# Gathered value rows summed on GpSimd instead of VectorE, with routing rounds written out and all first-layer rows gathered in the first layer

## The chip, the cores and the metric

The kernel runs on one core of one Trainium2 chip. The metric is the device time of one execution in microseconds; lower is better. PE is TensorE, DVE is VectorE, ACT is ScalarE, POOL is GpSimd and SP is SyncE, whose queue carries the weight loads.

## What is computed

A decoder block on 256 tokens of width 2048 in float32. The change touches only its last part, the expert channel mixer ("peer"). Each token and head picks 16 of 16384 experts by product keys. Each expert has one row in `u_tab` (first layer) and one in `v_tab` (second layer):

```python
s1 = einsum('thd,hnd->thn', qp[..., :half], sub_k1)      # 128 scores
s2 = einsum('thd,hnd->thn', qp[..., half:], sub_k2)      # 128 scores
v1, i1 = top_k(s1, 16);  v2, i2 = top_k(s2, 16)
cand = (v1[..., :, None] + v2[..., None, :]).reshape(T, 8, 256)
vals, flat = top_k(cand, 16)
experts = i1[flat // 16] * 128 + i2[flat % 16]
gates = softmax(vals)
hid = gelu(einsum('cd,chkd->chk', x, u_tab[experts]))
out = einsum('chk,chkd->cd', gates * hid, v_tab[experts])
```

## The kernel before

**Two ways for the tokens.** For 224 of the 256 tokens both expert layers are computed densely on PE: every expert's row is used for every token, and a table of gates that is zero for experts not picked selects. For the other 32 tokens (G = 32) the picked rows are gathered from HBM by indices: 32 tokens x 128 picks = 4096 rows of each table, 128 at a time, so 32 gathers of 128 x 2048 of the u rows (GJ = 32, numbers 0 to 31) and 32 of the v rows (numbers 32 to 63). A gather is an indirect DMA that POOL issues (`gather`, L488). Each u gather is multiplied by the tokens' normalised input and summed along the row on DVE (`gathered`, L1792), which gives one dot product per row; each v gather is scaled by its weight (one number per partition) and added to `y_acc`, also on DVE (L1795 for the first, L1798 for the rest: a multiply and an add in one instruction).

**The two dense layers.** Each streams 128 units of 128 x 2048 weights (1 MB each) through SP's queue. ACT rounds a unit to `w_hi` (`hi_wide`, L575), DVE subtracts to get the remainder `w_lo` (`lo_wide`, L1392), and PE multiplies with both. Four slots of `w_hi`/`w_lo` exist (SPLIT = 4), so the split of unit n+3 starts when unit n starts. The loops run over i = 0 to 15, with eight units k = 0 to 7 in each.

**First layer** (`hidden`, PE lines L1255 and L1256). While units stream, DVE also does the routing for i = 0 to 7 (`route`, two of the 16 routing rounds in each i; for each round part 0 copies 256 scores `sc` to `s_now`, L1719, and takes the top 16 of the first half, L1701 to L1705; part 1 takes those of the second half; part 2 those of the 256 sums; part 3 turns positions into one-hot rows `hot`). POOL finishes each round (`lookup`, L471 to L476) and adds two product halves for every second unit (`hidden_sum`, L467). In i = 1 to 5 DVE runs this as a hardware loop with the round number in a register. From i = 8 (I_TAB) on DVE builds gate tables (`picks_hot`, L1748 and L1752), which PE multiplies out (L1282), and reduces gathered u rows at the slots `PRE_SLOTS`, 27 of them (PRE = 27), over two buffers (`pre_ring`).

**Second layer** (PE lines L1304 and L1305, from 1643.7 us). For each pair of units, number m, the right-hand operand is made first: DVE multiplies the activations `h_in` by the gates `g_tab` (L1803), ACT rounds the product to `w_ul` (L867), and DVE subtracts (L1806). The two halves of `w_ul` alternate, so this chain for pair m+1 runs while PE works on pair m, and PE's wait for it is `wlow_done`. DVE's program is in order: at even k a `w_lo`, then the chain's product and difference; at odd k a `w_lo`. ACT's is in order too: at even k a `w_hi`, then the chain's rounding; at odd k a `w_hi`. POOL waits at each m until the chain m-1 is done, then loads the next `h_in` (L459), at even m also the next `g_tab` (L462), and at some m gathers the next row into `ring` (three buffers). DVE takes gathered rows behind a `w_lo` at the slots `V_SLOTS`: the 5 remaining u rows and the 32 v rows, three in each i. Where PE needs `y_acc` is only the very end (`bank_turned`, wait for `ring_used` 64).

Of the kernel before, what the change touches and what calls it, by code (L numbers as in the profile page):

```python
# [69 lines left out]
PRE = 27  # L70
# [25 lines left out]
def hybrid_block(nc, io):  # L96

    ctx = ExitStack()
    with ctx:
# [253 lines left out]
        def _(pool):  # L353
# [196 lines left out]
        def _(act):  # L550
# [355 lines left out]
            for i in range(1):  # L906
                experts_out(i)
            experts_out(1, gelu=7)
            with act.Fori(2, U_IT // 2 - 1) as i:
# [1085 lines left out]
```

## Time and profile before

| | us |
|---|---|
| median of three runs | 2315.85 (2314.83 to 2316.34) |
| profiled execution, its own time | 2314.72 |
| its span in the trace | 2312.7 |
| first expert layer, PE's stretch in the trace | about 946 to 1643.7 |
| second expert layer | 1643.7 to about 2286 |
| tail after it | about 27 |

The trace is that of the execution of 2314.72 us; 2.0 us of it lie outside the span. A row of the page's fifth part or of a query by groups gives a source line, the engine, the operation, output and inputs, how many, busy time and mean duration, and then the engine's idle time in front of them with what ended it. A row of a timeline gives start, duration, engine, line, operation and, in brackets, idle time in front with its releaser.

### The profile page before, as it was taken

To read this page: it belongs to the slowest core of one execution; us is meant where nothing else is said; L and a number is where in the kernel's file an instruction comes from. 1 tells how busy PE (TensorE), PEld (TensorE's weight loads), DVE (VectorE), ACT (ScalarE), POOL (GpSimd) and SP (SyncE) were. 2 spreads that over 40 slices of the span, in tenths; PEclk is the share of its full clock that TensorE was granted. 3 is DMA by queue.
4 is the path that set the end of the run, shared out by engine and by line. 5 is a ranking of instruction groups with operands and counts; after the bars stand their busy time and mean duration, and the time that the engine had idled before them with its cause. 6 is when DMAs were issued, how large, how long until landed. Compare 5 with 4: busy or idle time off the path is not lost.

```text
span 2312.7 us, 36297 instructions
## 1 busy us (share of the span) xinstructions
PE 2278.0 (98%) x13406; PEld 2072.4 (90%) x13406; DVE 1684.5 (73%) x2065; ACT 1214.2 (53%) x1138; POOL 476.6 (21%) x430
## 2 busy tenths in 40 slices
PE   7999999999999999999999999999999999999997
PEld 6888888888888889999999999999999999899997
DVE  5544776565655555989889989897688888888765
ACT  5534555555454344666666666565544444444443
POOL 0001342100000000243344422222222322222000
PEclk9999999999999999999999999999999999999999
DMA  7756555545456656666666899998999999999882
GB/s 279 276 192 216 207 204 209 196 164 174 166 201 222 225 199 234 211 226 228 222 235 229 318 343 336 326 331 317 356 383 366 377 382 376 370 397 379 327 305 83
DMA packets 122281, 623.70 MB, mean 270 GB/s; under 512 B 12000, under 2 KB 40928, under 8 KB 61776
## 3 DMA queue, kind: packets, MB, share of 16 engines
q1 hardware_dynamic: 58752, 423.65, 49.8%
q0 software_dynamic: 25616, 156.65, 17.9%
q10 hardware_dynamic: 37824, 42.18, 5.1%
q8 instruction: 60, 0.98, 0.2%
q14 instruction: 29, 0.24, 0.0%
HBM read 576.29 MB, written 46.14 MB: 269 GB/s over the span
## 4 chain that ended last, share of the span: by engine, by line
PE 79%; DVE 12%; issue 6%; ACT 1%; DMA 1%; DVEq 0%; POOL 0%; ACTq 0%; SPq 0%; POOLq 0%
PE psum L1304 17%; PE psum L947 10%; PE psum L949 10%; PE psum L948 10%; PE psum L1255 9%; PE psum L1305 8%; PE psum L1256 4%; DVE w_lo L1392 4%; PE psum L1282 2%; PE psum L1081 1%; DVE s_now L1719 1%; PE psum L1042 1%; DMA w_raw<-in_w_units 1%; PE psum L1003 1%; DVE i_top L1705 1%
## 5 line engine op out<-in xcount | busy, mean ns | idle before, releaser
L1255 PE MATMUL psum<-h2T,w_hi 128*128 128x448 f32 x2048 | 646.0, 374 | 1.4 <-DVE w_lo L1392 1.4
L1304 PE MATMUL psum<-w_ul,w_hi 128*128 128x448 f32 x2048 | 643.2, 374 | 3.5 <-DVE w_ul L1806 3.5
L1256 PE MATMUL psum<-h2T,w_lo 128*128 128x224 f32 x2048 | 543.3, 265 | 0.0
L1305 PE MATMUL psum<-w_ul,w_lo 128*128 128x224 f32 x2048 | 541.2, 264 | 0.0
L1384 DVE TENSOR_TENSOR w_lo<-w_raw,w_hi 128x2048 fp32r<-128x2048 f32 x144 | 332.2, 2312 | 214.9 <-ACT w_hi L563 214.5
L1304 PEld LDWEIGHTS psum<-w_ul,w_hi 128*128 128x128 f32 x2048 | 384.1, 188 | 34.1 <-issue 4.2
L563 ACT ACTIVATE w_hi<-w_raw 128x2048 fp32r<-128x2048 f32 x144 | 275.5, 1913 | 264.1 <-DMA w_raw<-in_w_units 231.6
L1255 PEld LDWEIGHTS psum<-h2T,w_hi 128*128 128x128 f32 x2048 | 383.8, 187 | 33.5 <-issue 3.7
L1305 PEld LDWEIGHTS psum<-w_ul,w_lo 128*128 128x128 f32 x2048 | 390.7, 191 | 0.0
L1256 PEld LDWEIGHTS psum<-h2T,w_lo 128*128 128x128 f32 x2048 | 390.2, 191 | 0.0
L1392 DVE TENSOR_TENSOR w_lo<-w_raw,w_hi 128x2048 fp32r<-128x2048 f32 x128 | 295.5, 2310 | 65.5 <-ACT w_hi L575 62.5
L1392 DVE TENSOR_TENSOR w_lo<-raw_x,w_hi 128x2048 fp32r<-128x2048 f32 x128 | 297.1, 2327 | 62.5 <-ACT w_hi L575 58.8
L947 PE MATMUL psum<-w_hi,hT_hi 128*128 128x512 f32 x768 | 306.1, 399 | 12.7 <-DVE w_lo L1384 12.7
L949 PE MATMUL psum<-w_hi,hT_lo 128*128 128x512 f32 x768 | 300.1, 391 | 0.0
L948 PE MATMUL psum<-w_lo,hT_hi 128*128 128x512 f32 x768 | 299.6, 390 | 0.0
L575 ACT ACTIVATE w_hi<-w_raw 128x2048 fp32r<-128x2048 f32 x128 | 244.5, 1913 | 82.4 <-PE psum L1305 36.9
L575 ACT ACTIVATE w_hi<-raw_x 128x2048 fp32r<-128x2048 f32 x128 | 243.4, 1907 | 49.4 <-PE psum L1305 28.7
L867 ACT ACTIVATE w_ul<-h_in 128x896 fp32r<-128x896 f32 x64 | 61.0, 954 | 271.3 <-DVE h_in L1803 271.3
L467 POOL TENSOR_TENSOR hs<-hs 128x448 f32<-128x448 f32 x64 | 110.7, 1730 | 385.4 <-ACT hs L856 378.7
L947 PEld LDWEIGHTS psum<-w_hi,hT_hi 128*128 128x128 f32 x768 | 144.7, 188 | 42.2 <-issue 14.0
L949 PEld LDWEIGHTS psum<-w_hi,hT_lo 128*128 128x128 f32 x768 | 144.5, 188 | 31.1
L948 PEld LDWEIGHTS psum<-w_lo,hT_hi 128*128 128x128 f32 x768 | 144.9, 189 | 28.4
(334 smaller groups left out, 2815.0 us busy)
## 6 DMA issues: line engine op xcount, KB each, us to landing
w_raw<-in_w_units SPq DMA_DIRECT2D x272, 1024.0 KB
raw_x<-in_w_units SPq DMA_DIRECT2D x128, 1024.0 KB, 6.7
g_tab<-tab_scratch POOLq DMA_DIRECT2D x32, 896.0 KB, 8.5
h_in<-hid_scratch POOLq DMA_DIRECT2D x64, 448.0 KB
hid_scratch<-hst ACTq DMA_DIRECT2D x32, 448.0 KB, 4.5
tab_scratch<-gate_a ACTq DMA_DIRECT2D x14, 1024.0 KB, 7.0
proj_scratch<-evac ACTq DMA_DIRECT2D x24, 512.0 KB, 4.9
x_nat<-in_x POOLq DMA_DIRECT2D x2, 2048.0 KB, 9.3
```

Of the source, the lines that this page charges most:

```text
L467: pool.tensor_tensor(both, both, hs[:, q, :, NU:2 * NU], ALU.add).then_inc(hid_summed, 1)
L563: act.activation(w_hi[:, s % SPLIT, :], w_raw[:, s % RAW, :], ACT.Copy).then_inc(hi_done, 1)
L575: act.activation(w_hi[:, s % SPLIT, :], src, ACT.Copy).then_inc(hi_done, 1)
L947: pe.matmul(out, xh[:, kc0 + c, ts], rh, start=st, stop=False, skip_group_check=True)
L948: pe.matmul(out, xh[:, kc0 + c, ts], rl, start=False, stop=False, skip_group_check=True)
L949: ins = pe.matmul(out, xl[:, kc0 + c, ts], rh, start=False, stop=en, skip_group_check=True)
L1255: pe.matmul(psum[:, k % 4, 0:2 * NU].rearrange("p (a t) -> p a t", a=2), uh, h2T[:, c, :, G:S], start=c == 0, stop=False, skip_group_check ...
L1256: ins = pe.matmul(psum[:, k % 4, NU:2 * NU], ul, h2T[:, c, 0, G:S], start=False, stop=c == KC - 1, skip_group_check=True)
L1304: pe.matmul(psum[:, c, 0:2 * NU].rearrange("p (a t) -> p a t", a=2), w_hi[:, s, o:o + P], ul, start=first, stop=False, skip_group_check=True)
L1305: return pe.matmul(psum[:, c, 0:NU], w_lo[:, s, o:o + P], ul[:, 0, :], start=False, stop=False, skip_group_check=True)
L1384: dve.tensor_tensor(w_lo[:, s % SPLIT, :], w_raw[:, s % RAW, :], w_hi[:, s % SPLIT, :].bitcast(F32), ALU.subtract).then_inc(lo_done, 1)
L1392: dve.tensor_tensor(w_lo[:, s % SPLIT, :], src, w_hi[:, s % SPLIT, :].bitcast(F32), ALU.subtract).then_inc(lo_done, 1)
```

## The change

Four things are edited.

1. The routing rounds of i = 1 to 5 are written out on DVE instead of looped, and the copy to `s_now` is gone: the top-16 search reads `sc` itself.
2. All 32 u gathers are reduced in the first layer (PRE = 32). Five of them are taken early, during routing, at slots (5,3), (5,7), (6,3), (6,7) and (7,3), all through one buffer; the gather indices (`gather_rows`) are made at (4,2) instead of (6,0). POOL's loop is written out from i = 4 for that. The other 27 keep their slots.
3. The 32 v rows are scaled and summed by POOL (`row_added`) in two instructions: a multiply by the row's weight in place, and an add to `y_acc` (the first row needs the multiply alone).
4. `V_SLOTS` has 32 entries, two in each i (k = 1 and 5) and a third (k = 7) in i = 2, 6 and 10; they only say at which m POOL takes a row and gathers the next. DVE takes no rows in the second layer. The gelu of the 32 dot products moves from unit (1,7) to (0,1) on ACT.

```diff
-PRE = 27
+PRE = 32
+PRE_EARLY = 5
...
+PRE_ISSUE = {(4, 3): 0, (5, 2): 1, (6, 0): 2, (6, 2): 3, (7, 0): 4}
+PRE_BUFFER = [0 if n < PRE_EARLY else (n - PRE_EARLY + 1) % 2 for n in range(PRE)]
-V_SLOTS = [(0, 5), (0, 7)] + [(i, k) for i in range(1, U_IT) for k in (1, 3, 5) if (i, k) != (2, 1)]
+V_SLOTS = sorted([(0, 5)] + [(i, k) for i in range(1, U_IT - 1) for k in (1, 5)] + [(2, 7), (6, 7), (10, 7)])
...
+            def row_added(n):
+                j = n % GJ
+                row = ring[:, (n - PRE) % RING, :]
+                if j == 0:
+                    pool.wait_ge(hidg_done, 1)
+                    pool.tensor_tensor(wts_g[:, :], hid_g[:, :], gsel[:, 2, :], ALU.mult).then_inc(hidg_done, 1)
+                    wait_alone(pool, hidg_done, 2)
+                pool.wait_ge(ring_in[(n - PRE) % RING], 16 * ((n - PRE) // RING + 1))
+                if j == 0:
+                    pool.tensor_scalar(y_acc[:, :], row, wts_g[:, 0:1], None, ALU.mult).then_inc(ring_used, 1)
+                else:
+                    pool.tensor_scalar(row, row, wts_g[:, j:j + 1], None, ALU.mult).then_inc(hidg_done, 1)
+                    wait_alone(pool, hidg_done, 2 + j)
+                    wait_alone(pool, ring_used, n)
+                    pool.tensor_tensor(y_acc[:, :], row, y_acc[:, :], ALU.add).then_inc(ring_used, 1)
...
+                    if (i, j) in PRE_ISSUE:
+                        pool.wait_ge(gidx_done, 1)
+                        gather(PRE_ISSUE[i, j])
...
-                if row < 2 * GJ and m in issue_at:
-                    gather(row)
-                    row += 1
+                if m in issue_at:
+                    row_added(added)
+                    added += 1
+                    if row < 2 * GJ:
+                        gather(row)
+                        row += 1
...
-                    if part == 0:
-                        step(dve.tensor_copy(s_now[:, :, :].rearrange("p a n -> p (a n)"), sc[:, ds(u, 1), :].rearrange("p a n -> p (a n)")), alone=True)
-                    top16(s_now[:, part, :], s_cut[:, part, :], v_top[:, part, :], i_top[:, part, :])
+                    top16(sc[:, u, part * PEER_NK:(part + 1) * PEER_NK], s_cut[:, part, :], v_top[:, part, :], i_top[:, part, :])
...
-                elif j == 0:
-                    dve.tensor_scalar(y_acc[:, :], row, wts_g[:, 0:1], None, ALU.mult).then_inc(ring_used, 1)
-                else:
-                    dve.wait_ge(ring_used, n)
-                    dve.scalar_tensor_tensor(y_acc[:, :], row, wts_g[:, j:j + 1], y_acc[:, :], ALU.mult, ALU.add).then_inc(ring_used, 1)
...
-            with dve.Fori(1, I_PICK0) as i:
-                step.enter(i, 1, 2 * ROUTE)
-                hidden(i, routes=True)
-                step.leave(I_PICK0 - 1)
-            for i in range(I_PICK0, I_TAB):
+            for i in range(1, I_TAB):
                 hidden(i, routes=True)
```

POOL in the second layer, before: `h_in` and `g_tab` are the pair's loads, `ring` is a gathered row.

```order
L459 DMA h_in<-hid_scratch 128x896
L462 DMA g_tab<-tab_scratch 128x1792
L459 DMA h_in<-hid_scratch 128x896
L488 DMA ring<-in_v_rows,gidx 128x2048
L459 DMA h_in<-hid_scratch 128x896
```

POOL at the same place in the changed program: `wts_g` holds the rows' weights, `y_acc` the running sum.

```order
L462 DMA h_in<-hid_scratch 128x896
L465 DMA g_tab<-tab_scratch 128x1792
L462 DMA h_in<-hid_scratch 128x896
L504 TENSOR_SCALAR ring<-ring,wts_g 128x2048
L507 TENSOR_TENSOR y_acc<-ring,y_acc 128x2048
L491 DMA ring<-in_v_rows,gidx 128x2048
```

A scaling and a sum have moved in front of the gather, and with it in front of the next pair's `h_in` load.

DVE in the second layer, before: `w_lo` is the remainder of a weight unit, `h_in` and `w_ul` are the operand chain of the pair.

```order
L1392 TENSOR_TENSOR w_lo<-w_raw,w_hi 128x2048
L1798 SCALAR_TENSOR_TENSOR y_acc<-ring,wts_g,y_acc 128x2048
L1392 TENSOR_TENSOR w_lo<-w_raw,w_hi 128x2048
L1803 TENSOR_TENSOR h_in<-h_in,g_tab 128x896
L1806 TENSOR_TENSOR w_ul<-h_in,w_ul 128x4x224
L1392 TENSOR_TENSOR w_lo<-raw_x,w_hi 128x2048 x2
```

DVE at the same place in the changed program.

```order
L1422 TENSOR_TENSOR w_lo<-raw_x,w_hi 128x2048 x2
L1813 TENSOR_TENSOR h_in<-h_in,g_tab 128x896
L1816 TENSOR_TENSOR w_ul<-h_in,w_ul 128x4x224
L1422 TENSOR_TENSOR w_lo<-w_raw,w_hi 128x2048 x2
L1813 TENSOR_TENSOR h_in<-h_in,g_tab 128x896
```

The row sums have left; the remainders and the operand chain stand as they did.

## Rows read from the trace of the kernel before

**Rows 1.** The page's busy times: engine, busy us, share of span, instructions.

```profile
PE 2278.0 (98%) x13406; PEld 2072.4 (90%) x13406; DVE 1684.5 (73%) x2065; ACT 1214.2 (53%) x1138; POOL 476.6 (21%) x430
```

**Rows 2.** Busy us by stretch: PE, PEld, DVE, ACT, POOL; clock, DMA share, GB/s.

```profile
960.00:1272.00 312.00, 310.64 (x1968) 293.69 (x1968) 281.85 (x587) 203.34 (x184) 132.28 (x107) 1.00 0.63 224
1272.00:1644.00 372.00, 371.21 (x2500) 356.14 (x2499) 319.52 (x387) 223.05 (x149) 95.95 (x67) 1.00 0.91 326
1644.00:1966.00 322.00, 321.20 (x2049) 306.12 (x2048) 258.66 (x158) 150.47 (x103) 85.25 (x75) 1.00 0.97 379
1966.00:2286.00 320.00, 317.30 (x2021) 301.94 (x2021) 241.46 (x146) 145.65 (x99) 54.43 (x58) 1.00 0.86 329
```

**Rows 3.** PE's waits: us in total, times, longest.

```profile
PE psum L1304 <- DVE w_ul L1806: 3.5, 5, 1.8
PE psum L1255 <- DVE w_lo L1392: 1.4, 5, 0.4
PE psum L1282 <- DVE hot2a L1752: 0.8, 1, 0.8
```

**Rows 4.** Timeline, one pair of the second layer without a gathered row: ACT, DVE, POOL.

```profile
2220.34 1.92 ACT L575 ACTIVATE w_hi<-w_raw 128x2048 fp32r<-128x2048 f32 x1 [1.99 <-PE psum L1305]
2225.62 0.95 ACT L867 ACTIVATE w_ul<-h_in 128x896 fp32r<-128x896 f32 x1 [3.36 <-DVE h_in L1803]
2226.48 1.90 ACT L575 ACTIVATE w_hi<-raw_x 128x2048 fp32r<-128x2048 f32 x1
2230.37 1.92 ACT L575 ACTIVATE w_hi<-raw_x 128x2048 fp32r<-128x2048 f32 x1 [1.99 <-PE psum L1305]
...
2222.29 2.29 DVE L1392 TENSOR_TENSOR w_lo<-w_raw,w_hi 128x2048 fp32r<-128x2048 f32 x1 [1.62 <-ACT w_hi L575]
2224.50 1.08 DVE L1803 TENSOR_TENSOR h_in<-h_in,g_tab 128x896 f32<-128x896 f32 x1
2226.61 1.09 DVE L1806 TENSOR_TENSOR w_ul<-h_in,w_ul 128x896 fp32r<-128x896 f32 x1 [1.02 <-ACT w_ul L867]
2228.41 2.29 DVE L1392 TENSOR_TENSOR w_lo<-raw_x,w_hi 128x2048 fp32r<-128x2048 f32 x1 [0.71 <-ACT w_hi L575]
...
2227.99 0.54 POOL L459 DMA_DIRECT2D h_in<-hid_scratch  x1 [8.96 <-DVE w_ul L1806]
```

**Rows 5.** Timeline, two places where POOL and DVE compute at once.

```profile
957.88 4.71 POOL L496 TENSOR_TENSOR g<-g,x_rep 128x2048 f32<-128x2048 f32 x1 [5.27 <-DMA x_rep<-x_scratch]
...
955.81 2.29 DVE L1392 TENSOR_TENSOR w_lo<-w_raw,w_hi 128x2048 fp32r<-128x2048 f32 x1 [0.17 <-DVE i_top L1705]
958.02 4.60 DVE L1724 CAST if_top<-i_top 128x32 f32<-128x32 uint32 x1
...
1140.41 1.16 POOL L467 TENSOR_TENSOR hs<-hs 128x448 f32<-128x448 f32 x1
...
1140.44 3.27 DVE L1392 TENSOR_TENSOR w_lo<-raw_x,w_hi 128x2048 fp32r<-128x2048 f32 x1 [0.24 <-DVE i_top L1705]
```

**Rows 6.** Timeline in a routing round: POOL's lookup and DVE's copy.

```profile
1257.30 3.21 POOL L471 TENSOR_TENSOR hot<-hot,if_top 128x512 f32<-128x512 f32 x1 [3.49 <-DVE hot L1734]
...
1257.07 2.28 DVE L1392 TENSOR_TENSOR w_lo<-raw_x,w_hi 128x2048 fp32r<-128x2048 f32 x1
1259.28 1.38 DVE L1719 COPY s_now<-sc 128x256 f32<-128x256 f32 x1
```

**Rows 7.** Timeline, an indirect gather beside a DVE subtraction, and one with DVE idle.

```profile
1684.03 2.73 POOL L488 DMA_INDIRECT ring<-in_u_rows,gidx  x1 [0.30 <-issue]
...
1683.61 2.29 DVE L1392 TENSOR_TENSOR w_lo<-raw_x,w_hi 128x2048 fp32r<-128x2048 f32 x1 [0.71 <-ACT w_hi L575]
...
1427.76 0.95 POOL L488 DMA_INDIRECT pre_ring<-in_u_rows,gidx  x1
```

**Rows 8.** Groups of DVE from 1080 us on: gathered rows.

```profile
L1798 DVE SCALAR_TENSOR_TENSOR y_acc<-ring,wts_g,y_acc 128x2048 f32<-128x2048 f32 x31 | 72.7, 2346 | 0.0
L1792 DVE CUSTOM_DVE_ANT_0 ring<-ring,g 128x2048 f32<-128x2048 f32 x5 | 11.4, 2285 | 0.0
```

More of the change, by code:

```diff
@@ L86, in bank_count @@
     return 2 * (KC // 2 - 1) + j + 1
-I_PICK0, I_TAB, I_PICK1, I_END = 6, 8, 9, 15
-PRE_SLOTS = [(I_TAB + (2 * n + 5) // 8, (2 * n + 5) % 8) for n in range(PRE)]
-V_SLOTS = [(0, 5), (0, 7)] + [(i, k) for i in range(1, U_IT) for k in (1, 3, 5) if (i, k) != (2, 1)]
+I_ROWS, I_PICK0, I_TAB, I_PICK1, I_END = 4, 6, 8, 9, 15
+PRE_SLOTS = [(5, 3), (5, 7), (6, 3), (6, 7), (7, 3)] + [(I_TAB + (2 * n + 5) // 8, (2 * n + 5) % 8) for n in range(PRE - PRE_EARLY)]
+PRE_ISSUE = {(4, 3): 0, (5, 2): 1, (6, 0): 2, (6, 2): 3, (7, 0): 4}
+PRE_BUFFER = [0 if n < PRE_EARLY else (n - PRE_EARLY + 1) % 2 for n in range(PRE)]
+V_SLOTS = sorted([(0, 5)] + [(i, k) for i in range(1, U_IT - 1) for k in (1, 5)] + [(2, 7), (6, 7), (10, 7)])
 VB = 4
@@ L481, in gather @@
                 if n < PRE:
-                    dst, landed, behind = pre_ring[:, n % 2, :], pre_in[n % 2], n - 1
+                    dst, landed, behind = pre_ring[:, PRE_BUFFER[n], :], pre_in[PRE_BUFFER[n]], n if n < PRE_EARLY else n - 1
                 else:
@@ L499, in _ @@
             pool.wait_ge(iota_in, 16)
-            with pool.Fori(0, I_TAB) as i:
+            with pool.Fori(0, I_ROWS) as i:
                 for j in range(4):
@@ L504, in _ @@
                         lookup(i * 2 + j // 2)
-            pool.wait_ge(gidx_done, 1)
-            pool.wait_ge(routed, ROUTES)
+            for i in range(I_ROWS, I_TAB):
+                for j in range(4):
+                    hidden_sum(i * 4 + j, j % 2)
+                    if j % 2 == 1:
+                        lookup(i * 2 + j // 2)
+                    if (i, j) in PRE_ISSUE:
+                        pool.wait_ge(gidx_done, 1)
+                        gather(PRE_ISSUE[i, j])
             for i in range(I_TAB, I_END):
@@ L509, in _ @@
                     hidden_sum(i * 4 + j, j % 2)
-                    if (i - I_TAB) * 4 + j < PRE:
-                        gather((i - I_TAB) * 4 + j)
+                    n = PRE_EARLY + (i - I_TAB) * 4 + j
+                    if n < PRE:
+                        if n == PRE_EARLY:
+                            pool.wait_ge(routed, ROUTES)
+                        gather(n)
             hidden_sum(4 * I_END, 0)
@@ L532, in _ @@
             issue_at = [4 * i + (k + 1) // 2 + 2 for i, k in V_SLOTS]
+            added = PRE
             for m in range(2, 2 * V_ROUNDS):
@@ L904, in gathered_gelu @@
                 act.activation(hid_g[:, :], dots[:, :], ACT.Gelu_apprx_tanh, scale=rs_g[:, 0:1]).then_inc(hidg_done, 1)
[L906 to L909, printed above, removed]
+            experts_out(0, gelu=1)
+            with act.Fori(1, U_IT // 2 - 1) as i:
                 experts_out(i)
@@ L1776, in gathered @@
             def gathered(n):
[L1778 to L1784 removed]
+                row = pre_ring[:, PRE_BUFFER[n], :]
+                dve.wait_ge(pre_in[PRE_BUFFER[n]], 16 * PRE_BUFFER[:n + 1].count(PRE_BUFFER[n]))
                 if n == 0:
                     dve.wait_ge(hg_done, 1)
[L1787 to L1798 removed]
+                dve.tensor_tensor_reduce(row, row, hg[:, :], 1.0, 0.0, ALU.mult, ALU.add, dots[:, n:n + 1]).then_inc(ring_used, 1)
             def weights(m, half):
@@ L1823, in hidden @@
                     lo_wide(i * 8 + (U0 + k + AHEAD), k + AHEAD)
-                    if k == 0 and isinstance(i, int) and i == I_PICK0:
+                    if (i, k) == (I_ROWS, 2):
                         gather_rows()
@@ L1865, in experts_out @@
                         weights(m, m % 2)
-                    if (i, k) in row_slots:
-                        gathered(row_slots[i, k])
-            row_slots = dict(zip(V_SLOTS, range(PRE, 2 * GJ)))
             def clear_tokens(h):
```

19 lines of the change are left out of this document (2 added, 17 removed).

## Prediction

> **What bounds the kernel now.** I read the page's busy times first, then the stretches, then PE's waits, then the timeline around one pair of units. PE is busy 2278.0 of 2312.7 us [rows 1], and in the two expert layers 1320.3 of 1326 us at the full granted clock, 1.00 [rows 2]. All that PE waits for DVE there is 3.5 + 1.4 + 0.8 = 5.7 us [rows 3]. So whatever this change takes off DVE can give back 5.7 us at most, 0.25% of the time. It can cost far more, since the engines that feed PE have little room in the second layer.
>
> How little is read from one pair [rows 4]. Let t = 0 be 2220.34, where ACT starts the rounding that it owes at the start of an even unit; the next pair starts at 10.03. DVE's remainder runs from 1.95 to 4.24, the product ends at 5.24, ACT's rounding at 6.23, the difference at 7.36, and PE needs it at 10.03. **The slack of the operand chain is 2.67 us.** At 7.65 POOL issues the next `h_in` load, until 8.19; DVE's odd remainder runs from 8.07 to 10.36. The next even remainder can start at 10.03 + 1.95 = 11.98.
>
> **What POOL and DVE do to each other.** An add of POOL over 128x2048 runs from 957.88 to 962.59 [rows 5]. It starts while a DVE subtraction still runs (to 958.10), and a DVE cast of 32 elements issued at 958.02 ends at 962.62, with the add. So the add had something to itself for 4.49 us from the end of the subtraction, and a tiny DVE operation waited all of it. The second place is the same with a DVE subtraction: 3.27 us instead of 2.29, ending about 2.1 us after POOL's 1.16 us add. I call this thing the port: one of the two holds it for a whole instruction. Who gets it next is in [rows 6]: POOL asked at 1257.30, DVE's subtraction ended at 1259.35, DVE's copy had been issued at 1259.28, and POOL went first: POOL ends at 1260.51, the copy at 1260.66. First asked, first served. The operations that this change meets in the second layer, remainder, product and difference, all read two SBUF tensors like the subtraction of [rows 5].
>
> **The change part by part.**
>
> *Value rows leave DVE.* 31 multiply-adds of 2.35 us and 5 dot products of 2.29 [rows 8], 84 us, leave the second layer's DVE. They stand behind PE, so this saves only the 3.5 us that PE waits for `w_ul` [rows 3].
>
> *Value rows come to POOL.* 31 adds at 4.49 us [rows 5] and 32 scalings. No row shows a scaling on POOL. From above it is bounded by the add, 4.49, which reads one tensor more. I take half of that, 2.25, since it reads one tensor and not two. Whether it needs the port is not shown either; the nearest row is the indirect gather, which reads one column of indices: alone 0.95 us, beside a subtraction 2.73 us [rows 7], ending 0.86 us after the subtraction's end at 1685.90. A single read of POOL waits for DVE too, so I take yes. From below its cost is then that of a scaling beside DVE's work, nothing, which is the first rival.
>
> Now one row, at a pair that starts at 0. POOL is ready to scale at about 8.3, behind its load. DVE's remainder has the port to 10.36; the scaling has it to 12.6; the next remainder (ready at 11.98) to 14.85; the add, ready at 12.8, was first in the queue and has it to 19.3. Only then the product, to 20.4, the rounding, to 21.4, and the difference, to 22.5. PE wants it at 20.06 and waits 2.45 us. After the first such row the odd remainder too comes late and the wait grows to what the port allows. Two pairs with one row need 4 x 2.29 + 4 x 1.09 = 13.5 us for DVE, 2.25 + 4.49 = 6.7 for POOL, and the gaps in which DVE waits for ACT, 2 x (1.02 + 0.71) = 3.5 [rows 4]: 23.7 us, where PE needs 20.06. **Each row costs 3.6 us.** At i = 2, 6 and 10 a third row follows in the next pair: there one pair carries a row, 6.75 + 6.74 + 1.73 = 15.2 against 10.03, 5.2 us each for six rows. The first row is a scaling alone and delays a remainder by 0.6 us, inside the slack: nothing. Sum: 24 x 3.6 + 6 x 5.2 + 2.45 = 120 us. It lies on PE's path, since nothing else covers a late `w_ul`.
>
> The Trainium skill ("GPSIMD Engine Reference", sections "4.1 Engine selection" and "3.1 Elementwise — side-by-side cycle accounting") calls GpSimd's one-input operations roughly line-rate, 1.03 cycles an element at 1.2 GHz: an estimate of 1.76 us for this scaling, and 0.49 us less for each of 31 rows, 105 us in place of 120. No row here shows a scaling on POOL. The same page's "8. Key points" names the contention: the interfaces are shared, and DVE instructions with two SBUF inputs or in a two-port mode meet it; [rows 5] agree, with 4.60 us for the cast.
>
> What is queued behind the row on POOL is the gather and the next `h_in` load, and behind that DVE's product. POOL is done with the row at 19.3, the gather at about 22, and the load is issued when the late difference is done, at 22.8; that `h_in` is wanted only a pair and a half later, so it isn't late.
>
> *Routing.* Each of the 16 rounds loses a copy of 1.38 us, of which some 1.1 us was waiting for POOL [rows 6]. Over i = 1 to 7 that is 14 x 1.38 = 19.3 us less for DVE, and the five early dot products add 5 x (2.29 + 0.08) = 11.8. DVE is busy 281.85 of 312 us there [rows 2] and PE waits for it 1.4 us, and 0.8 us at the first table [rows 3]. At best these 2.2 us go. At worst, if what the copies free in i = 1 to 4 isn't kept as lead, i = 5 to 7 stand at 11.8 - 6 x 1.38 = 3.5 us more, and PE waits for that before the first table. The remainders are made up to three units ahead, so lead is kept: I take -1.5, range -2.2 to +3.5. An early gather has about two units between issue and use; if it lands late, DVE waits in order and spends the same lead.
>
> *The rest.* Writing out the loop adds no work; the moved index making, the earlier gelu and the different buffer order shift small operations whose results have units of room. Nothing.
>
> **Sum.** +120 - 3.5 - 1.5 = +115 us. On the profiled execution, 2314.72, that is 2430; on the median, 1.1 us higher, 2431.
>
> **The rivals.**
>
> *The scaling needs no port.* It then runs beside the odd remainder and only the add blocks: 13.5 + 4.49 + 3.5 = 21.5 for two pairs, 1.4 us a row, and 12.97 for one, 2.9 us for six rows: 24 x 1.4 + 6 x 2.9 = 51, and with the other terms +46: 2362. For it speaks that no row shows a one-input computation waiting; against it the gather of [rows 7].
>
> *The scaling is as slow as the add.* 2.24 us more for each of 31 rows: 120 + 69 - 5 = +184, 2500. Against it speaks that it reads half as much.
>
> *POOL gives way (the other side).* If POOL's long add stood aside whenever DVE asks, the rows would fill DVE's idle time and cost PE nothing; PE's 5.7 us could go: 2311. It decides where POOL's uninterrupted hold falls below the slack of 2.67 us; between that and nothing gained lies "no difference". Against it stand both places of [rows 5], 4.49 us uninterrupted.
>
> *DVE's share of the add is smaller than the queue says,* because DVE's instruction, issued already, sometimes goes first, as the order of arrival is tight around 10.36 and 14.85. The sum over the port then still binds unless the gaps are filled: filled wholly, 13.5 + 6.7 = 20.2 against 20.06, close to nothing a row, 2320; half filled, 1.9 us a row and some 65 us in all, 2376.
>
> **How the numbers follow.** The queue with a scaling on the port, 2431 (between 2400 and 2475): 0.66. No port for the scaling, 2362: 0.13. Gaps partly filled, 2340 to 2400: 0.08. Slow scaling, around 2500: 0.05. POOL gives way, faster: 0.05. No difference: 0.03. A measurement of this kernel tells about 0.2% from no change, 4.6 us. The range 2355 to 2475 leaves out the slow scaling, the last two and part of the filled gaps. Faster 0.05, same 0.03, slower 0.92.
>
> **What would show it.** PE's wait for the difference in `w_ul` (was 3.5 us in 5 times) should be about 120 us in some 31 times of 2.5 to 5.2. The second layer should last some 755 us, not 640, the first layer within 3 us of before, at an unchanged clock. POOL's adds should stand at 4.5 us and more, the scalings at 2 to 4.5 with waiting, DVE's products and remainders in row pairs at 4 to 6 us where POOL holds. I am wrong if DVE's product keeps its 1.08 us beside POOL's add, if the scaling doesn't lengthen anything of DVE, or if PE waits for `w_lo` instead, which would mean that a chain I left out, the loads behind late remainders, comes last.

## The result, and the profile after

The changed kernel takes 2466.64 us (median of 4 runs, 2465.22 to 2467.52) where the kernel before took 2315.41 on the same chip: ratio 1.0649, interval 1.0637 to 1.0662, 151 us more. The predicted 2431 had the sign and the mechanism and was 36 us short.

In the changed kernel the lines have moved: the first layer's PE line L1255 is L1285, the second layer's L1304 and L1305 are L1334 and L1335, the remainder L1392 is L1422, the product L1803 is L1813, the difference L1806 is L1816, ACT's roundings L575 and L867 are L607 and L899, and POOL scales at L504 and adds at L507.

The page's busy times, to be held against [rows 1]:

```profile
PE 2337.5 (95%) x13406; PEld 2121.6 (86%) x13406; DVE 1831.6 (74%) x2016; ACT 1211.8 (49%) x1138; POOL 817.7 (33%) x494
```

Two numbers deserve a stop. DVE has 49 instructions fewer, with some 84 us of rows gone from the second layer, and is busy 147 us longer. PE has the same 13406 matmuls and is busy 59.5 us longer. DVE's "busy" holds waiting that the profile doesn't separate; PE's holds matmuls at the lower clock. By stretches, with the columns of [rows 2]:

```profile
960.00:1272.00 312.00, 310.61 (x1984) 296.04 (x1983) 277.21 (x581) 204.90 (x187) 145.59 (x113) 1.00 0.68 242
1272.00:1644.00 372.00, 369.89 (x2488) 354.40 (x2487) 318.50 (x386) 221.68 (x146) 96.02 (x67) 1.00 0.91 325
1644.00:2020.00 376.00, 332.89 (x1941) 312.67 (x1940) 310.69 (x122) 143.28 (x95) 230.43 (x97) 0.92 0.75 296
2020.00:2440.00 420.00, 369.32 (x2152) 346.78 (x2152) 343.16 (x143) 153.18 (x108) 238.00 (x96) 0.92 0.68 265
```

The first layer is as it was: PE's stretch in it lasts 701.1 us before and 700.5 now, to 1644.4. All the time is in the second, where PE got through 2049 matmuls in 322 us before [rows 2] and now through 1941 in 376. To the last matmul with `w_hi` the second layer took 650.7 us and takes 801.7, the whole 151. PE's waits, as in [rows 3]:

```profile
PE psum L1334 <- DVE w_ul L1816: 93.8, 32, 4.5
PE psum L1312 <- DVE hot2a L1778: 1.9, 1, 1.9
PE psum L1285 <- DVE w_lo L1422: 1.6, 2, 1.4
```

93.8 us are waits for the operand chain. The rest is in the matmuls: L1334 takes 399 ns in the mean, where its twin took 374 before. Groups of 1660 to 2440 us:

```profile
L1334 PE MATMUL psum<-w_ul,w_hi 128*128 128x448 f32 x1992 | 682.9, 399 | 93.0 <-DVE w_ul L1816 93.0
L1422 DVE TENSOR_TENSOR w_lo<-raw_x,w_hi 128x2048 fp32r<-128x2048 f32 x62 | 319.9, 5185 | 39.8 <-ACT w_hi L607 39.5
L504 POOL TENSOR_SCALAR ring<-ring,wts_g 128x2048 f32<-128x2048 f32 x31 | 189.8, 6122 | 1.1
L507 POOL TENSOR_TENSOR y_acc<-ring,y_acc 128x2048 f32<-128x2048 f32 x31 | 144.4, 4657 | 6.6 <-POOL ring L504 6.6
L1813 DVE TENSOR_TENSOR h_in<-h_in,g_tab 128x896 f32<-128x896 f32 x62 | 96.6, 1558 | 1.1 <-DMA h_in<-hid_scratch 1.1
L1816 DVE TENSOR_TENSOR w_ul<-h_in,w_ul 128x896 fp32r<-128x896 f32 x62 | 94.1, 1518 | 63.2 <-ACT w_ul L899 63.2
```

The 62 remainders from `raw_x`, two of the four in a cycle and the two that mostly meet POOL's row, take 5.19 us each where [rows 4] have 2.29: 180 us of DVE "work" that is standing still. POOL's queue isn't what is late: DVE waits only 1.1 us in all for `h_in` to land. And here is one settled cycle of two pairs with one row, POOL, DVE and ACT, from one late end of the chain (2106.40) to the next (2131.21):

```profile
2115.59 5.46 POOL L504 TENSOR_SCALAR ring<-ring,wts_g 128x2048 f32<-128x2048 f32 x1
2121.27 4.68 POOL L507 TENSOR_TENSOR y_acc<-ring,y_acc 128x2048 f32<-128x2048 f32 x1 [0.21 <-POOL ring L504]
...
2105.31 1.09 DVE L1816 TENSOR_TENSOR w_ul<-h_in,w_ul 128x896 fp32r<-128x896 f32 x1 [1.01 <-ACT w_ul L899]
2107.11 4.49 DVE L1422 TENSOR_TENSOR w_lo<-w_raw,w_hi 128x2048 fp32r<-128x2048 f32 x2 [0.71 <-ACT w_hi L607]
2111.53 1.08 DVE L1813 TENSOR_TENSOR h_in<-h_in,g_tab 128x896 f32<-128x896 f32 x1
2113.63 1.09 DVE L1816 TENSOR_TENSOR w_ul<-h_in,w_ul 128x896 fp32r<-128x896 f32 x1 [1.02 <-ACT w_ul L899]
2115.44 12.66 DVE L1422 TENSOR_TENSOR w_lo<-raw_x,w_hi 128x2048 fp32r<-128x2048 f32 x2 [0.71 <-ACT w_hi L607]
2128.02 1.08 DVE L1813 TENSOR_TENSOR h_in<-h_in,g_tab 128x896 f32<-128x896 f32 x1
2130.12 1.09 DVE L1816 TENSOR_TENSOR w_ul<-h_in,w_ul 128x896 fp32r<-128x896 f32 x1 [1.02 <-ACT w_ul L899]
...
2118.28 1.92 ACT L607 ACTIVATE w_hi<-raw_x 128x2048 fp32r<-128x2048 f32 x1 [2.88 <-PE psum L1335]
```

Two remainders beside POOL's two instructions take 12.66 us, not 4.49; the other two take 4.49. Nothing else in the cycle is longer. It lasts 24.8 us, where PE would need 20.06. In DVE's brackets ("idle before") there is only ACT: 1.02 + 0.71 + 1.02 + 0.71 us. ACT waits once for PE, but its rounding ends at 2120.20, while DVE is still at the remainder before, which alone lasts 6.04 us, until 2121.48. So no wait for PE reaches the end of the chain: **DVE, ACT and POOL form a loop of their own, and PE trails it.**

### The profile page after: what moved, and what is told of

Read it like the earlier page. It is cut to its first block, busy times and chain, and to the rows that moved or that the text cites. A ratio compares the mean times of both kernels' runs of the same rounds, so it can differ in the third digit from the quotient of the medians.

```text
span 2464.3 us, 36030 instructions
## 1 busy us (share of the span) xinstructions
PE 2337.5 (95%) x13406; PEld 2121.6 (86%) x13406; DVE 1831.6 (74%) x2016; ACT 1211.8 (49%) x1138; POOL 817.7 (33%) x494
## 4 chain that ended last, share of the span: by engine, by line
PE 69%; DVE 17%; issue 8%; ACT 4%; DMA 1%; DVEq 0%; ACTq 0%; POOL 0%; SPq 0%; POOLq 0%
PE psum L1285 15%; DVE w_lo L1422 10%; PE psum L977 10%; PE psum L979 10%; PE psum L978 10%; PE psum L1286 7%; PE psum L1334 6%; ACT w_hi L607 3%; DVE h_in L1813 3%; PE psum L1335 3%; PE psum L1312 2%; DVE w_ul L1816 1%; PE psum L1111 1%; ACT w_ul L899 1%; PE psum L1236 1%
## 5 line engine op out<-in xcount | busy, mean ns | idle before, releaser
L1334 PE MATMUL psum<-w_ul,w_hi 128*128 128x448 f32 x2048 | 701.1, 398 | 93.8 <-DVE w_ul L1816 93.8
L1285 PE MATMUL psum<-h2T,w_hi 128*128 128x448 f32 x2048 | 644.4, 373 | 1.6 <-DVE w_lo L1422 1.6
L1335 PE MATMUL psum<-w_ul,w_lo 128*128 128x224 f32 x2048 | 563.8, 275 | 0.0
L1334 PEld LDWEIGHTS psum<-w_ul,w_hi 128*128 128x128 f32 x2048 | 412.5, 201 | 136.6 <-DVE w_ul L1816 81.8
L1422 DVE TENSOR_TENSOR w_lo<-raw_x,w_hi 128x2048 fp32r<-128x2048 f32 x128 | 473.2, 3709 | 72.6 <-ACT w_hi L607 70.2
L1335 PEld LDWEIGHTS psum<-w_ul,w_lo 128*128 128x128 f32 x2048 | 419.0, 205 | 0.0
L1285 PEld LDWEIGHTS psum<-h2T,w_hi 128*128 128x128 f32 x2048 | 383.8, 187 | 31.6 <-issue 2.1
L1422 DVE TENSOR_TENSOR w_lo<-w_raw,w_hi 128x2048 fp32r<-128x2048 f32 x128 | 292.4, 2304 | 60.9 <-ACT w_hi L607 58.2
L607 ACT ACTIVATE w_hi<-raw_x 128x2048 fp32r<-128x2048 f32 x128 | 244.1, 1909 | 97.8 <-PE psum L1335 79.2
L607 ACT ACTIVATE w_hi<-w_raw 128x2048 fp32r<-128x2048 f32 x128 | 241.7, 1907 | 50.0 <-PE psum L1286 24.6
L899 ACT ACTIVATE w_ul<-h_in 128x896 fp32r<-128x896 f32 x64 | 60.9, 952 | 404.2 <-DVE h_in L1813 404.2
L504 POOL TENSOR_SCALAR ring<-ring,wts_g 128x2048 f32<-128x2048 f32 x31 | 189.8, 6122 | 1.1
```

Source lines behind the costliest of these rows:

```text
L504: pool.tensor_scalar(row, row, wts_g[:, j:j + 1], None, ALU.mult).then_inc(hidg_done, 1)
L607: act.activation(w_hi[:, s % SPLIT, :], src, ACT.Copy).then_inc(hi_done, 1)
L1285: pe.matmul(psum[:, k % 4, 0:2 * NU].rearrange("p (a t) -> p a t", a=2), uh, h2T[:, c, :, G:S], start=c == 0, stop=False, skip_group_check ...
L1334: pe.matmul(psum[:, c, 0:2 * NU].rearrange("p (a t) -> p a t", a=2), w_hi[:, s, o:o + P], ul, start=first, stop=False, skip_group_check=True)
L1335: return pe.matmul(psum[:, c, 0:NU], w_lo[:, s, o:o + P], ul[:, 0, :], start=False, stop=False, skip_group_check=True)
L1422: dve.tensor_tensor(w_lo[:, s % SPLIT, :], src, w_hi[:, s % SPLIT, :].bitcast(F32), ALU.subtract).then_inc(lo_done, 1)
```

## The experiments

The theory to test: one of DVE and POOL holds a port for a whole instruction, so a row costs the two holds less what slack is left. "Hold" is the time for which POOL keeps DVE from its operands; "duration" is the length of POOL's own record. Open were how long each instruction holds it, whether duration or hold counts, and what the lowered clock costs.

**The rows alone.** The changed kernel, with only the value rows given back to DVE, at the new `V_SLOTS`:

```diff
-                    row_added(added)
-                    added += 1
...
+                    if (i, k) in row_slots:
+                        summed(row_slots[i, k])
```

> The changed kernel with one part undone: the 32 value rows are summed on DVE again, at the new slots (two in an i, three in i = 2, 6 and 10); the written-out routing and the five early dot products stay. Port theory (POOL's scaling and add keep DVE from its operands, and nothing else costs): the whole of the 151 us goes, 2312 to 2318. Rival, that the first-layer edits or the gather order carry part of it: over 2330.

Measured: 2311.70 us, ratio to the kernel before 0.9981 (0.9972 to 0.9991). So the port theory stands: the value rows on POOL cost 155 us, and all the rest of the change together gains 4.7 us (2.1 to 6.5 by the interval). PE's wait for the operand chain here:

```profile
PE psum L1315 <- DVE w_ul L1811: 1.8, 3, 0.8
```

**Each instruction alone.** The sum without the scaling, and the scaling without the sum:

```diff
 add alone
-                    pool.tensor_scalar(row, row, wts_g[:, j:j + 1], None, ALU.mult).then_inc(hidg_done, 1)
...
 scaling alone
-                    pool.tensor_tensor(y_acc[:, :], row, y_acc[:, :], ALU.add).then_inc(ring_used, 1)
```

> The changed kernel without POOL's scaling: gathered value rows are added unscaled, so the weighting of these rows is left out. Port theory: two pairs need 13.5 us of DVE, 4.5 of POOL and 3.5 of gaps for ACT, 21.5 against 20.06, 1.4 us a row and 2.9 where two pairs in a row carry one: about +46, 2355 to 2372, PE's single waits 1 to 3 us. Clock theory (each wait of PE lets the granted clock fall and the slow matmuls add to the time): 20 us or more on top, over 2380.

> The changed kernel without POOL's add: rows are only scaled in place, so the sum of the value rows is left out. The scaling took 5.46 us even with DVE off SBUF, yet DVE's product came through about 3.4 us after its start. If it holds the port for those 3.4 to 3.7 us: 13.5 + 3.6 + 3.5 = 20.6 for two pairs, 0.5 us a row, 2 us in six: 2325 to 2345. If it holds it for all of its 5.46 us: 22.5, 2.4 us a row and 3.9 in six, 2380 to 2400.

Measured: 2358.40 us with the add alone (ratio 1.0180, 1.0159 to 1.0200), 2332.79 with the scaling alone (1.0069, 1.0049 to 1.0089). Both lie where the port theory had them. A hold of the full 5.46 us (2380 to 2400) fell, and so did the clock theory (over 2380): with the add alone PE waits for `w_ul` 31 times too, 36.5 us in all and 2.7 at most, and the granted clock over the span is 0.995. Over the 2311.70 of the experiment before that is 46.7 and 21.1 us; together they cost 155, more than twice the 68 of the two alone. The slack of a cycle of two pairs explains that, 20.06 - 13.5 - 3.5 = 3.1 us: each alone has it to itself, both together have it once. Two remainders beside a 5.48 us scaling, with no add, POOL and DVE of the scaling alone:

```profile
2101.27 5.48 POOL L504 TENSOR_SCALAR ring<-ring,wts_g 128x2048 f32<-128x2048 f32 x1
...
2101.11 8.26 DVE L1419 TENSOR_TENSOR w_lo<-raw_x,w_hi 128x2048 fp32r<-128x2048 f32 x2 [0.72 <-ACT w_hi L604]
```

DVE loses 8.26 - 4.49 = 3.8 us to an instruction of 5.48. So the scaling is longer than the add, but holds the port for less than its length.

**Holds by themselves.** A small kernel of its own, executed once: two equal instructions of POOL over 128x2048, alone and beside six dependent ones of DVE. The sections of POOL beside DVE's subtractions, and of POOL's scaling beside DVE's, come twice in it, with the same times.

> A measuring kernel of its own: nothing of the block is computed, the output is zeros. POOL runs each operation twice, alone and beside six dependent DVE operations: scaling by a pointer or by a constant, multiply by a broadcast weight, add, copy, of 2048 and 512 columns; DVE's are a subtraction of two SBUF tiles, a scaling, a subtraction with a PSUM operand and a max. Port theory: alone the scaling by pointer takes 5.46 us, add 4.5, copy about 2 to 3; beside the subtraction each POOL operation delays one DVE subtraction by its hold, add by 4.5, scaling by 3.4 to 3.7; the max and the PSUM subtraction are delayed by none. Rival, POOL slows every DVE operation by a rate: all of DVE's stretch a little.

POOL alone (scaling by a column, multiplication by the same column spread out, add x2, copy x2):

```profile
15.34 5.44 POOL L26 TENSOR_SCALAR pa<-pa,pw 128x2048 f32<-128x2048 f32 x1 [0.17 <-POOL pa L26]
39.10 7.34 POOL L32 TENSOR_TENSOR pa<-pa,pw 128x2048 f32<-128x2048 f32 x2 [0.24 <-DVEq L61]
49.14 9.13 POOL L35 TENSOR_TENSOR pb<-pa,pb 128x2048 f32<-128x2048 f32 x2 [0.24 <-DVEq L61]
61.41 3.91 POOL L38 COPY pb<-pa 128x2048 f32<-128x2048 f32 x2 [0.24 <-DVEq L61]
```

DVE: six subtractions alone; beside POOL's scaling, spread multiplication, add and copy; then, beside scalings, six of DVE's own scalings, six subtractions with a PSUM operand and six top-8 searches:

```profile
67.06 13.92 DVE L41 TENSOR_TENSOR dc<-da,db 128x2048 f32<-128x2048 f32 x6 [57.57 <-POOLq L61]
81.20 7.53 DVE L44 TENSOR_SCALAR dc<-da 128x2048 f32<-128x2048 f32 x6 [0.22 <-POOLq L61]
...
117.24 20.70 DVE L41 TENSOR_TENSOR dc<-da,db 128x2048 f32<-128x2048 f32 x6 [0.22 <-DVEq L88]
...
158.93 20.64 DVE L41 TENSOR_TENSOR dc<-da,db 128x2048 f32<-128x2048 f32 x6 [0.22 <-DVEq L88]
179.79 22.43 DVE L41 TENSOR_TENSOR dc<-da,db 128x2048 f32<-128x2048 f32 x6 [0.22 <-DVEq L88]
202.44 17.20 DVE L41 TENSOR_TENSOR dc<-da,db 128x2048 f32<-128x2048 f32 x6 [0.22 <-DVEq L88]
219.87 17.77 DVE L44 TENSOR_SCALAR dc<-da 128x2048 f32<-128x2048 f32 x6 [0.22 <-DVEq L88]
237.86 13.89 DVE L47 TENSOR_TENSOR dc<-da,ps 128x2048 f32<-128x2048 f32 x6 [0.22 <-DVEq L88]
251.97 13.94 DVE L50 MAX8 top<-da 128x8 f32<-128x2048 f32 x6 [0.22 <-DVEq L88]
```

DVE isn't slowed evenly, as the rival had it. The third of the six subtractions beside the scaling, and the last three:

```profile
125.28 5.68 DVE L41 TENSOR_TENSOR dc<-da,db 128x2048 f32<-128x2048 f32 x1
...
131.00 6.94 DVE L41 TENSOR_TENSOR dc<-da,db 128x2048 f32<-128x2048 f32 x3
```

The second and the third take 5.69 and 5.68 us, the other four 2.29. So each POOL instruction stops one subtraction, and half of what DVE loses is the hold of one POOL instruction against this subtraction:

| POOL instruction | alone, us | DVE's subtractions lose, us |
|---|---|---|
| scaling by a column | 5.44 | (20.70 - 13.92) / 2 = 3.4 |
| multiply by the spread column | 3.67 | (20.64 - 13.92) / 2 = 3.4 |
| add | 4.56 | (22.43 - 13.92) / 2 = 4.25 |
| copy | 1.95 | (17.20 - 13.92) / 2 = 1.6 |

DVE's own scalings, which read one SBUF tensor, lose (17.77 - 7.53) / 2 = 5.1 us to each of POOL's scalings, not 3.4. So the hold belongs to a pair of instructions, one on each engine; "port" is a name for what they share, and no row shows the part itself. The subtraction that reads PSUM and the search lose nothing: their 13.89 and 13.94 are their times alone.

**Duration or hold.** The two ways to scale hold alike and differ in length by 1.8 us. In the kernel:

```diff
-                    pool.tensor_scalar(row, row, wts_g[:, j:j + 1], None, ALU.mult).then_inc(hidg_done, 1)
+                    pool.tensor_tensor(row, row, wts_g[:, j:j + 1].to_broadcast([P, D]), ALU.mult).then_inc(hidg_done, 1)
```

> The changed kernel with POOL's scaling written as a tensor_tensor multiply by the weight broadcast along the row, which reads two inputs. Expected to take 4.5 us like the add and to hold the port for all of it. Port theory: the hold counts, 4.5 in place of some 3.6, so it is slower than the changed kernel although the instruction is shorter: 2480 to 2500. Rival, the duration on POOL counts: 1 us a row less, 2430 to 2445.

Measured: 2466.77 us, ratio 1.0647 (1.0626 to 1.0669): the same time as the changed kernel, so both expectations missed. POOL's groups from 1660 us on:

```profile
L507 POOL TENSOR_TENSOR y_acc<-ring,y_acc 128x2048 f32<-128x2048 f32 x31 | 197.3, 6366 | 6.3 <-POOL ring L504 6.3
L504 POOL TENSOR_TENSOR ring<-ring,wts_g 128x2048 f32<-128x2048 f32 x31 | 116.4, 3755 | 0.5
```

The scaling is 2.4 us shorter than in the changed kernel, the add behind it 1.7 us longer, and the cycle doesn't move. With the small kernel's 3.4 us for either form this leaves the hold, and not the duration, as what counts. I had written down a longer hold for this form because it has two inputs; that was wrong.

**Smaller pieces.** If holds compete with DVE's chain, shorter ones can slip into the 3.5 us of gaps. Each row in two halves of 1024 columns, scaling and add in turn:

```diff
+                    for q in range(PIECES):
+                        b = slice(q * (D // PIECES), (q + 1) * (D // PIECES))
+                        pool.tensor_scalar(row[:, b], row[:, b], wts_g[:, j:j + 1], None, ALU.mult).then_inc(hidg_done, 1)
...
+                        pool.tensor_tensor(y_acc[:, b], row[:, b], y_acc[:, b], ALU.add).then_inc(hidg_done, 1)
...
```

> The changed kernel with each row's scaling and add cut into halves of 1024 columns, in the order scale, add, scale, add: same columns, four shorter holds of about 1.8 and 2.3 us, each below the slack of 2.67 us. If what counts is the single hold against the slack: close to before, 2315 to 2340. If what counts is the sum of the holds over the port (DVE 13.5, POOL 8, gaps 3.5 in 20.06 us): no gain, 2450 to 2480.

Measured: 2400.67 us, ratio 1.0369 (1.0350 to 1.0388), between the two expectations, so both missed. A cycle of two pairs lasts 22.2 us, not 24.8: of the 4.7 us above PE's 20.06 some 2.6 are gone, the rest stays. DVE's four remainders in the cycle that ends at 2124.04:

```profile
2102.54 7.83 DVE L1427 TENSOR_TENSOR w_lo<-raw_x,w_hi 128x2048 fp32r<-128x2048 f32 x2 [0.71 <-ACT w_hi L612]
2114.19 6.73 DVE L1427 TENSOR_TENSOR w_lo<-w_raw,w_hi 128x2048 fp32r<-128x2048 f32 x2 [0.71 <-ACT w_hi L612]
```

They lose 3.34 + 2.24 = 5.6 us to four POOL instructions, where the whole ones cost 12.66 - 4.49 = 8.2. One by one: the two half adds cost 2.19 and 2.24 us, together what the whole add does (6.70 - 2.29 = 4.4). The saving is all in the scaling. Its second half costs DVE nothing: it is on POOL from 2108.21 to 2114.00, and the product and the difference in that stretch keep their 1.08 and 1.09. Its first half costs 3.43 - 2.29 = 1.1 us, where the whole scaling costs 6.04 - 2.29 = 3.75. So shorter instructions do slip into gaps, and a half scaling holds for less than half of a whole one; I had put 1.8 for it. And a wait appeared that the changed kernel doesn't have, at i = 2, 6 and 10, where three rows follow in neighbouring pairs. POOL and DVE at the first of them:

```profile
1807.54 0.59 POOL L463 DMA_DIRECT2D h_in<-hid_scratch  x1
...
1817.93 2.34 DVE L1818 TENSOR_TENSOR h_in<-h_in,g_tab 128x896 f32<-128x896 f32 x1 [9.12 <-issue]
```

The `h_in` load could have been issued at 1801.38, when the difference ended, but stands behind a row and its gather on POOL until 1807.54; the product starts 10.4 us later, which is also the median landing of these loads there. Three such waits of 9.1 to 9.2 us on DVE, 27.5 us, stand among the 89 us that this version still loses against the rows on DVE.

**What the low clock costs.** After each wait PE runs at about half clock for 3 us. Windows of 3 us in the changed kernel, granted clock behind the busy times:

```profile
2103.00:2106.00 3.00, 0.44 (x4) 0.16 (x2) 1.99 (x3) 1.67 (x2) 1.22 (x1) 1.00 0.42 142
2106.00:2109.00 3.00, 2.54 (x9) 2.37 (x10) 2.29 (x2) 2.88 (x2) 1.11 (x2) 0.55 1.03 434
2109.00:2112.00 3.00, 3.00 (x18) 2.86 (x18) 3.00 (x3) 0.00 (x0) 0.00 (x0) 0.88 0.98 399
2112.00:2115.00 3.00, 3.00 (x21) 2.86 (x21) 1.70 (x2) 2.35 (x2) 0.00 (x0) 1.00 1.03 434
```

That is the step from 2.4 to 1.2 GHz and back, once in 24.8 us. It looks like a cost of 50 us and more. To see whether it is one, PE was given twelve matmuls with a zero tile before every second wait for the chain:

```diff
+                    if k in (2, 6):
+                        zero = rs_diag[:, 1, :]
+                        for _ in range(FILL):
+                            pe.matmul(psum[:, 0, 0:P], zero, zero, start=False, stop=False, skip_group_check=True)
                     if k % 2 == 0:
                         pe.wait_ge(wlow_done, i * 4 + (k // 2 + 1))
...
```

Left out of the diff is where DVE sets the tile to zero and PE waits for that, once.

> The changed kernel with 12 matmuls of a zero tile (128x128, about 0.22 us each, 2.7 us, result unchanged) in front of PE's waits for the operand chain at k = 2 and 6, so that PE isn't idle while it waits. Theory that the lower clock is hidden (the loop of DVE, ACT and POOL sets 24.8 us for two pairs, and slow matmuls only shorten PE's next wait): clock near 1.00, time within 10 us of 2467. Clock theory: up to 58 us of slow matmuls go, 2410 to 2430.

Measured: 2469.11 us, ratio 1.0663 (1.0647 to 1.0679). The clock of both second-layer stretches rises from 0.92 to 0.97, short of the 1.00 expected, L1334's mean falls from 399 to 384 ns, the waits for `w_ul` fall from 93.8 to 48.6 us (part of them is now filled), and the time is what it was. The first of the two stretches:

```profile
1644.00:2020.00 376.00, 352.79 (x2287) 335.70 (x2286) 308.02 (x120) 143.03 (x95) 224.85 (x96) 0.97 0.74 293
```

The clock theory's 2410 to 2430 fell. What PE loses at the low clock it would otherwise lose waiting: a matmul that ends earlier only meets the late operand earlier.

**The routing edits alone, on the kernel before.** Rounds written out and copy gone; and rounds written out with the copy kept:

```diff
-                    if part == 0:
-                        step(dve.tensor_copy(s_now[:, :, :].rearrange("p a n -> p (a n)"), sc[:, ds(u, 1), :].rearrange("p a n -> p (a n)")), alone=True)
-                    top16(s_now[:, part, :], s_cut[:, part, :], v_top[:, part, :], i_top[:, part, :])
+                    top16(sc[:, u, part * PEER_NK:(part + 1) * PEER_NK], s_cut[:, part, :], v_top[:, part, :], i_top[:, part, :])
...
-            with dve.Fori(1, I_PICK0) as i:
...
+            for i in range(1, I_TAB):
```

> The kernel before with one part of the change alone: routing rounds written out and the copy of the scores gone; 27 early rows, 5 u rows and all value rows on DVE in the second layer as before. DVE loses 16 copies of 1.38 us where PE waits for it 1.4 us in all: 1 to 2 us faster than before, 2313 to 2315. Rival, the freed time is lost again to POOL's adds, which now meet DVE's subtraction: within 0.5 us of before.

> The kernel before with the routing rounds written out but the copy of 256 scores kept, all else as before. The routing edits together gave 4.8 us, more than the 2.2 us that the view of waits shows. Theory A: the gain is the copies', whose 14 x 1.38 us took DVE's lead at many small places, so this kernel stands within 1 us of the kernel before (2314.5 to 2316.5), and PE's matmul count in 940 to 1300 us stays near 2281. Rival B: the loop itself costs (instruction fetch, register work, waits at each turn), so this kernel keeps 2 us or more of the 4.8 (2310.4 to 2313.5), with some 2300 matmuls or more in that stretch.

Measured: 2310.43 us (ratio 0.9979, 0.9970 to 0.9988) and 2312.57 us (ratio 0.9984, 0.9975 to 0.9993): 4.8 us (2.8 to 6.9) and 3.4 us (1.6 to 5.8) faster than the kernel before. The first is more than the 1 to 2 us expected, so that expectation missed; the second is rival B's, the loop itself. The 1.4 us between them, the copies' share, is within the two intervals. In the traces the first layer lasts 701.1 us before, 696.0 with both edits and 697.7 with the loop written out alone. The stretch of 1000 to 1190 us, inside the looped part, of these three in this order:

```profile
1000.00:1190.00 190.00, 189.01 (x1196) 178.39 (x1195) 170.67 (x355) 123.40 (x111) 73.18 (x64) 1.00 0.63 229
...
1000.00:1190.00 190.00, 190.00 (x1215) 181.22 (x1214) 156.93 (x350) 125.71 (x113) 65.67 (x64) 1.00 0.65 231
...
1000.00:1190.00 190.00, 190.00 (x1215) 181.21 (x1214) 173.84 (x364) 125.98 (x115) 85.08 (x65) 1.00 0.66 231
```

PE's busy time says that 1.0 us can be won, its matmuls say more: 1215 in place of 1196, and 19 at 190 / 1215 = 0.156 us are 3.0 us. One of PE's waits of the kernel before shows what comes round there:

```profile
1072.71 0.44 PE L1255 MATMUL psum<-h2T,w_hi 128*128 128x448 f32 x1 [0.24 <-DVE w_lo L1392]
```

Four such waits stand 40.8 us apart (1031.89, 1072.71, 1113.54 and 1154.35), once in a turn of DVE's loop; each is 0.2 to 0.3 us as a wait and 0.75 us by the count. So most of what the late operand costs sat in matmuls that count as busy. Written out, both are gone, with the copies still there. What the copies add shows after the loop: with them PE still waits 1.0 us for `hot2a` at the first table, without them not at all. The copy gone with the loop kept wasn't tried. The version with both routing edits and all rows on DVE, 2310.43 us, beats both kernels; the rows on DVE at the new slots, with the early dot products (2311.70), can't be told from it.

## Why the prediction was right, and where it was short

**The mechanism** stands. DVE's losses with the rows on POOL, the cycle with no step of PE in it, and the 155 us that vanish when the rows go back to DVE are what it said. Its rule for who goes first, "first asked, first served", does not stand, as told below; no time of the loop hangs on it. Of its rivals, "POOL gives way" and "no port for the scaling" (2362) fell: the scaling alone costs 21 us, which it couldn't without the port. "As slow as the add" (2500) is the odd one: it was right on the duration, too low even, and wrong on the cost, because the hold is shorter than the duration. "Gaps partly filled" fell for whole rows; with half rows it is in part what happens. Its own figure was loose too: with half of the gaps filled a pair with its own row costs 6.75 + 6.74 + 0.87 - 10.03 = 4.3 us, so the sum is 24 x 1.9 + 6 x 4.3 + 2.45 = 74 us, not 65.

**The step that was mis-sized** is the scaling, 2.25 us, taken as half an add "since it reads one tensor and not two". It lasts 5.46 and holds the port for 3.4 by the small kernel, 3.75 by the 6.04 us of the remainder in the kernel. The bound from above, "the add, which reads one tensor more", wasn't a bound: the number of inputs doesn't order POOL's instructions, since the copy (one input) takes 1.95 and the scaling (one input and a column) 5.44. A value from the middle between two bounds that no row carries was a guess. The add's 4.49 was right within 0.25 (hold 4.25).

The page that I cited, "GPSIMD Engine Reference" of the Trainium skill, section "4.1 Engine selection", would have led further off: its roughly line-rate for one input gave an estimate of 1.76 us, against 5.46 measured; only the copy, 1.95, comes near that. Section "8. Key points" of the same page of the Trainium skill has contention with DVE instructions of two SBUF inputs or in a two-port mode. The small kernel agrees on the first: the subtraction of two SBUF tensors loses 3.4 us, the one with a PSUM operand nothing. DVE's scaling, with one SBUF input, loses 5.1; in which mode it ran no row shows.

With the measured holds the prediction's own sum reads: two pairs 13.5 + 3.4 + 4.25 + 3.5 = 24.6 us (24.8 measured), 4.6 a row, 24 x 4.6 = 110; a pair with its own row 6.75 + 7.65 + 1.73 = 16.1 against 10.03, 6 x 6.1 = 37; with 2.45 for the second row 149, less 5 makes +144, 2460. Measured are +151. So the formula, with holds measured in a kernel of their own, gives 95% of the cost, and one input of it was 1.15 us low, 31 times.

**Order.** "First asked, first served" fits the add of the cycle shown: at 2121.27 it found DVE at work until 2121.48, took 4.68 us, and the remainder begun at 2121.40 waited, 6.70 us. It doesn't fit the scaling. That begins at 2115.59, 0.15 us after the remainder, yet takes 5.46 us, about its time alone, and the remainder takes 6.04: the later one went first. The opposite stands at the neighbouring rows, POOL and DVE at i = 2:

```profile
1795.90 9.01 POOL L504 TENSOR_SCALAR ring<-ring,wts_g 128x2048 f32<-128x2048 f32 x1
...
1797.38 2.29 DVE L1422 TENSOR_TENSOR w_lo<-w_raw,w_hi 128x2048 fp32r<-128x2048 f32 x1
1799.59 4.53 DVE L1813 TENSOR_TENSOR h_in<-h_in,g_tab 128x896 f32<-128x896 f32 x1
```

The scaling had begun 1.5 us before this remainder and was passed by it; then the product waited. With the spread multiplication at the same place (begun 1795.68, remainder begun 1797.20) it is the remainder that waits, 5.69 us, so the kind of instruction has a part in it. POOL issues a load just in front of each scaling, from 2115.02 on in the cycle shown; whether that decides the first case is not shown, and what lets DVE pass in the second stays open. The sum of a cycle doesn't depend on the order, since both holds fall between two ends of the chain either way. The slack of 2.67 us can't be read from a cycle that has used it up. Where both holds met the two remainders, product and difference kept their 1.08 and 1.09; with the neighbouring rows their means rose to 1.56 and 1.52.

**Waits of PE.** I wrote about 120 us in 31 times of 2.5 to 5.2; it is 93.8 in 32, at most 4.5. The second layer was to grow by some 115 us and grew by 151. "At an unchanged clock" was wrong: it is 0.92 in the second layer. The two misses belong together. Of the 151 us, 90 show as more waiting and most of the rest as slower matmuls, (399 - 374) ns x 2048 = 51 us on L1334. Whoever had read only the waits would have found some 60 us missing, and would have sought them in a second cause; the filled waits show that the clock isn't one.

**The small terms.** -3.5 for the value rows off DVE and -1.5 for the routing were the forecast; the changed kernel with the rows on DVE gains 4.7 us, against 5. That this came out so near is in part luck: the interval is 2.1 to 6.5, and the parts were mis-sized. The traces place only some of it, since the two profiled executions differ by 1.6 us (2314.72 and 2313.14); there the second layer is 2.3 us shorter, 648.4 against 650.7. PE's stretch in the first layer is 0.6 us shorter in the changed kernel and 0.4 longer with the rows on DVE. It is 5.1 us shorter with the routing edits alone, where I had 2.2 as the most, since "writing out the loop adds no work" took no account of what the loop itself costs, and since "at best these 2.2 us go" took PE's waits for all of the loss. The rest of the first-layer edits, the five early dot products above all, takes 4.5 us back: the wait for `hot2a` grew from 0.8 to 1.9 us and one of 1.4 for `w_lo` came, at 1265 us. That DVE's lead is used up there is how I read it; no run has the early dot products alone. My bound of +3.5 assumed that no lead is kept, and was further off than -1.5.

**POOL's queue**: that the late load does no harm was right for the changed kernel and wrong in the version with halves, where it costs three waits of 9 us.

## What to carry to other kernels

Before moving work from DVE to POOL, add up on one line, for one period, DVE's instructions that meet POOL at the port (here those that read two SBUF tensors), POOL's holds, and DVE's gaps for other engines. Here that sum passed PE's period, 24.6 us against 20.06, and the excess was paid each time, while the page had DVE at 74% and POOL at 33%. Price a POOL instruction that no row shows by a small kernel, beside DVE and alone, since neither its number of inputs nor its length gives the hold. And where PE waits often, count its matmuls per stretch beside its busy time and its waits: here both of the latter hid late operands.

## What the hardware showed that was not expected

- POOL over 128x2048 in float32: scaling by a column 5.44 us, by a constant 5.36, multiplying by the same column spread out 3.67, add 4.56, copy 1.95. The slowest form is the one made for scaling.
- Against DVE's two-input subtraction the port is held by POOL for 3.4 us of the 5.44 of a scaling and for 4.25 of the add's 4.56.
- DVE's scaling, with one SBUF input and 1.26 us long, is hit harder by POOL's scaling (5.1 us each) than the two-input subtraction is (3.4).
- POOL's scaling passed a DVE remainder begun 0.15 us earlier, and was passed by one begun 1.5 us later.
- After waits of some 3 us, one in 24.8 us, PE's granted clock was half for 3 us each time, 0.92 in the mean, and giving part of it back (0.97) gained no time, since another loop set it.
- DVE's routing as a hardware loop, i = 1 to 5, cost 3.4 us (1.6 to 5.8) against the same instructions written out; PE's waits for it come once in a turn. Which part of a turn costs it was not measured.
